# Split weight blocks written over the raw block, six blocks ahead of TensorE

## The reference

```python
for l in range(DEPTH):                                     # DEPTH = 2
    proj = einsum('btd,de->bte', x, w_in[l])               # D_IN = 7168 columns
    ...
    y_conv = conv_mixer(...)                               # 31 taps, 512 channels
    y_hgrn = hgrn2_mixer(...)                              # gated recurrence, 6 heads of 128
    y_ret = retention_mixer(...)                           # 6 heads of 128
    h = einsum('bte,ed->btd', concatenate([y_conv, y_hgrn, y_ret]), w_out[l])
    x = layer_norm(ALPHA * x + h, ...)
    f = square(relu(einsum('btd,df->btf', x, w_ff1[l])))   # 2048 -> 8192
    h = einsum('btf,fd->btd', f, w_ff2[l])                 # 8192 -> 2048
    x = layer_norm(ALPHA * x + h, ...)
```

## Time and profile before

| | |
|---|---|
| time, median of 3 runs | 3781.74 us (3781.71 to 3783.3) |
| span of the profiled execution | 3784.1 us |
| TensorE busy | 3541.0 us (94%) |
| VectorE busy | 2168.7 us (57%) |
| ScalarE busy | 1618.5 us (43%) |
| GpSimd busy | 419.4 us (11%) |
| moved by DMA | 615.57 MB, mean 163 GB/s |

### The profile page before, as it was taken

How to read it: one execution, slowest core, us unless ns; L and a number is a source line. 1 busy time by engine, 2 the same in 40 slices (tenths; PEclk the granted TensorE clock), 3 DMA queues, 4 the chain that set the end, 5 groups by cost and what they waited for, 6 DMA issues and landing times.

```text
span 3784.1 us, 45287 instructions
## 1 busy us (share of the span) xinstructions
PE 3541.0 (94%) x16538; PEld 2940.2 (78%) x16538; DVE 2168.7 (57%) x2397; ACT 1618.5 (43%) x1953; POOL 419.4 (11%) x330
## 2 busy tenths in 40 slices
PE   7899989999999888989899999999999978999979
PEld 6677778887888766777788888888888777788767
DVE  4976564555555587665555545565447544645544
ACT  3444334343434335433444443444445433355543
POOL 0614000000000060140100000000000041000100
PEclk9999999999999999999999999999989889999989
DMA  6444456655565555445566666556646200565534
GB/s 224 137 150 148 163 173 186 195 185 182 185 188 184 165 151 149 134 150 187 203 190 188 192 186 192 185 187 193 194 136 175 87 6 31 165 193 169 160 104 134
DMA packets 310641, 615.57 MB, mean 163 GB/s; under 512 B 19082, under 2 KB 19113, under 8 KB 308539
## 3 DMA queue, kind: packets, MB, share of 16 engines
q1 hardware_dynamic: 306144, 591.73, 50.6%
q0 software_dynamic: 4320, 21.34, 1.8%
HBM read 610.90 MB, written 2.10 MB: 162 GB/s over the span
## 4 chain that ended last, share of the span: by engine, by line
PE 81%; DVE 13%; ACT 4%; issue 2%; DMA 0%; POOL 0%; SPq 0%; DVEq 0%; ACTq 0%
PE ps_unit L252 24%; PE ps_unit L254 24%; PE ps_unit L253 24%; DVE sb_w_lo L236 4%; DVE sb_conv_y L901 2%; PE ps_mix L2324 2%; ACT sb_w_hi L229 2%; PE ps_mix L975 1%; PE ps_mix L376 1%; PE ps_mix L530 1%; DVE sb_h_s L1167 1%; PE ps_mix L1995 1%; PE ps_mix L2322 0%; DMA sb_raw<-in_w_in_dram 0%; PE ps_mix L2679 0%
## 5 line engine op out<-in xcount | busy, mean ns | idle before, releaser
L236 DVE TENSOR_TENSOR sb_w_lo<-sb_raw,sb_w_hi 128x1024 fp32r<-128x1024 f32 x1120 | 1407.7, 1264 | 1311.6 <-ACT sb_w_hi L229 1305.9
L229 ACT ACTIVATE sb_w_hi<-sb_raw 128x1024 fp32r<-128x1024 f32 x1120 | 1183.1, 1060 | 1838.1 <-PE ps_unit L254 1823.6
L252 PE MATMUL ps_unit<-sb_w_hi,sb_a_hi 128*128 128x512 f32 x3456 | 1383.1, 400 | 87.1 <-DVE sb_w_lo L236 56.0
L253 PE MATMUL ps_unit<-sb_w_lo,sb_a_hi 128*128 128x512 f32 x3456 | 1361.4, 394 | 0.0
L254 PE MATMUL ps_unit<-sb_w_hi,sb_a_lo 128*128 128x512 f32 x3456 | 1361.1, 394 | 0.0
L252 PEld LDWEIGHTS ps_unit<-sb_w_hi,sb_a_hi 128*128 128x128 f32 x3456 | 660.1, 191 | 242.9 <-DVE sb_w_lo L236 49.5
L254 PEld LDWEIGHTS ps_unit<-sb_w_hi,sb_a_lo 128*128 128x128 f32 x3456 | 658.5, 191 | 141.3
L253 PEld LDWEIGHTS ps_unit<-sb_w_lo,sb_a_hi 128*128 128x128 f32 x3456 | 660.0, 191 | 132.8
L252 PE MATMUL ps_unit<-sb_w_hi,sb_f_hi 128*128 128x512 f32 x1024 | 399.9, 391 | 0.0
L254 PE MATMUL ps_unit<-sb_w_hi,sb_f_lo 128*128 128x512 f32 x1024 | 398.6, 389 | 0.0
L253 PE MATMUL ps_unit<-sb_w_lo,sb_f_hi 128*128 128x512 f32 x1024 | 398.4, 389 | 0.0
(11 more groups left out here) (455 smaller groups left out, 2142.7 us busy)
## 6 DMA issues: line engine op xcount, KB each, us to landing
sb_raw<-in_w_ff_dram SPq DMA_DIRECT2D x512, 512.0 KB, 3.8
sb_raw<-in_w_in_dram SPq DMA_DIRECT2D x224, 512.0 KB, 3.8
sb_raw<-in_e_w_in_dram SPq DMA_DIRECT2D x112, 512.0 KB, 3.6
sb_raw<-in_o_w_in_dram SPq DMA_DIRECT2D x112, 512.0 KB, 3.7
sb_raw<-in_w_out_dram SPq DMA_DIRECT2D x64, 512.0 KB, 4.4
sb_raw<-in_e_w_out_dram SPq DMA_DIRECT2D x32, 512.0 KB, 4.4
sb_raw<-in_o_w_out_dram SPq DMA_DIRECT2D x32, 512.0 KB, 4.7
sb_raw<-in_e_w_mem_kv_dram SPq DMA_DIRECT2D x16, 512.0 KB, 4.5
```

The lines of the kernel that those rows point to most:

```text
L229: k.nc.scalar.activation(k.w_hi[:, slot], k.raw[:, j], ACT.Copy).then_inc(k.hi_ready, 1)
L236: k.nc.vector.tensor_tensor(k.w_lo[:, slot], k.raw[:, j], k.w_hi[:, slot].bitcast(F32), ALU.subtract).then_inc(k.lo_ready, 1)
L252: k.nc.tensor.matmul(acc, hi[:, kt, tokens], w_hi, start=kt == 0, stop=False)
L253: k.nc.tensor.matmul(acc, hi[:, kt, tokens], w_lo, start=False, stop=False)
```

## The change

The low half of a block is written in place over the raw block, and the high half gets eight slots of its own, in the memory that both halves had before. SyncE's load of a slot now waits for TensorE to have finished the block eight earlier, which was the last reader of the slot. ScalarE's split no longer waits for TensorE: the load that it waits for implies it. The splits stand six blocks ahead of TensorE's place in the program in place of four, and the counts that start the semaphores follow (`block_done` begins at 8, `lo_ready` at 0).

```diff
-HI_SLOTS = 4
+AHEAD = 6
...
     k.raw = sb("raw", 0, [P, BLOCKS, KB, NC])
-    k.w_hi = sb("w_hi", 32 * K, [P, HI_SLOTS, KB, NC], F32R)
-    k.w_lo = sb("w_lo", 48 * K, [P, HI_SLOTS, KB, NC], F32R)
+    k.w_lo = sb("w_lo", 0, [P, BLOCKS, KB, NC], F32R)
+    k.w_hi = sb("w_hi", 32 * K, [P, BLOCKS, KB, NC], F32R)
...
 # sp_unit (and sp_feed_forward alike)
-        sp.wait_ge(k.lo_ready, b0 + (s * BLOCKS + j + 1))
+        sp.wait_ge(k.block_done, b0 + (s * BLOCKS + j + 1))
         sp.dma_start(k.raw[:, j], w[:, KB * j:KB * (j + 1), bass.ds(column, NC)]).then_inc(k.raw_ready[j], 16)
...
 # act_split
     act.wait_ge(k.raw_ready[j], b0 * 2 + 16 * (c // BLOCKS + 1))
-    act.wait_ge(k.block_done, b0 + (c + 1))
-    k.nc.scalar.activation(k.w_hi[:, slot], k.raw[:, j], ACT.Copy).then_inc(k.hi_ready, 1)
+    k.nc.scalar.activation(k.w_hi[:, j], k.raw[:, j], ACT.Copy).then_inc(k.hi_ready, 1)
...
 # dve_split
-    k.nc.vector.tensor_tensor(k.w_lo[:, slot], k.raw[:, j], k.w_hi[:, slot].bitcast(F32),
-                              ALU.subtract).then_inc(k.lo_ready, 1)
+    k.nc.vector.tensor_tensor(k.w_lo[:, j], k.raw[:, j], k.w_hi[:, j].bitcast(F32), ALU.subtract).then_inc(k.lo_ready, 1)
...
 # pe_block
-    pe.wait_ge(k.lo_ready, b0 + (BLOCKS + c + 1))
+    pe.wait_ge(k.lo_ready, b0 + (c + 1))
...
 # split_units; Meanwhile.ahead and the feed-forward loops alike
-            for c in range(HI_SLOTS, HI_SLOTS + BLOCKS):
-                if take and c == HI_SLOTS + BLOCKS - 1:
+            for c in range(AHEAD, AHEAD + BLOCKS):
+                if take and c == AHEAD + BLOCKS - 1:
...
 # wait_unit
-    eng.wait_ge(k.block_done, b0 + (HI_SLOTS + (s + 1) * BLOCKS))
+    eng.wait_ge(k.block_done, b0 + (s + 2) * BLOCKS)
...
 # start of the kernel, ScalarE and VectorE
-            for c in range(HI_SLOTS):
+            for c in range(AHEAD):
...
 # VectorE
-            dve.sem_inc(k.lo_ready, BLOCKS)
...
 # TensorE
-            pe.sem_inc(k.block_done, HI_SLOTS)
+            pe.sem_inc(k.block_done, BLOCKS)
```

More of the change, by code:

```diff
@@ L218, in sp_unit @@
     for j in range(BLOCKS):
-        sp.wait_ge(k.lo_ready, b0 + (s * BLOCKS + j + 1))
+        sp.wait_ge(k.block_done, b0 + (s * BLOCKS + j + 1))
         sp.dma_start(k.raw[:, j], w[:, KB * j:KB * (j + 1), bass.ds(column, NC)]).then_inc(k.raw_ready[j], 16)
 def act_split(act, k, b0, c):
-    j, slot = c % BLOCKS, c % HI_SLOTS
+    j = c % BLOCKS
     act.wait_ge(k.raw_ready[j], b0 * 2 + 16 * (c // BLOCKS + 1))
-    act.wait_ge(k.block_done, b0 + (c + 1))
-    k.nc.scalar.activation(k.w_hi[:, slot], k.raw[:, j], ACT.Copy).then_inc(k.hi_ready, 1)
+    k.nc.scalar.activation(k.w_hi[:, j], k.raw[:, j], ACT.Copy).then_inc(k.hi_ready, 1)
 def dve_split(dve, k, b0, c):
-    j, slot = c % BLOCKS, c % HI_SLOTS
+    j = c % BLOCKS
     dve.wait_ge(k.hi_ready, b0 + (c + 1))
-    k.nc.vector.tensor_tensor(k.w_lo[:, slot], k.raw[:, j], k.w_hi[:, slot].bitcast(F32),
-                              ALU.subtract).then_inc(k.lo_ready, 1)
+    k.nc.vector.tensor_tensor(k.w_lo[:, j], k.raw[:, j], k.w_hi[:, j].bitcast(F32), ALU.subtract).then_inc(k.lo_ready, 1)
 def pe_block(pe, k, b0, c, hi, lo):
-    s, j, slot = c // BLOCKS % 2, c % BLOCKS, c % HI_SLOTS
+    s, j = c // BLOCKS % 2, c % BLOCKS
     if j == 0:
         pe.wait_ge(k.evacuated, b0 + (c + BLOCKS))
-    pe.wait_ge(k.lo_ready, b0 + (BLOCKS + c + 1))
+    pe.wait_ge(k.lo_ready, b0 + (c + 1))
     for n in range(KB):
@@ L250, in pe_block @@
             acc = k.ps_unit[:, s, t, :]
-            w_hi, w_lo = k.w_hi[:, slot, n, :], k.w_lo[:, slot, n, :]
+            w_hi, w_lo = k.w_hi[:, j, n, :], k.w_lo[:, j, n, :]
             k.nc.tensor.matmul(acc, hi[:, kt, tokens], w_hi, start=kt == 0, stop=False)
@@ L309, in __init__ @@
         self.eng, self.k, self.block, self.take = eng, k, block, take
-        self.ahead = 0 if who == "pe" else HI_SLOTS
+        self.ahead = 0 if who == "pe" else AHEAD
         self.first = k.block0[who]
@@ L512, in sp_feed_forward @@
                     src = w2_groups[:, bass.ds(q, 1), rows, (u - 4) * NC:(u - 3) * NC].rearrange("p q kt n -> p (q kt) n")
-                sp.wait_ge(k.lo_ready, b0 + (u * BLOCKS + j + 1))
+                sp.wait_ge(k.block_done, b0 + (u * BLOCKS + j + 1))
                 sp.dma_start(k.raw[:, j], src).then_inc(k.raw_ready[j], 16)
@@ L574, in group @@
         for u in range(FF_UNITS):
-            for j in range(4, 8):
+            for j in range(AHEAD, AHEAD + 4):
                 act_split(act, k, b0, u * BLOCKS + j)
                 if between:
-                    between(u, j - 4)
+                    between(u, j - AHEAD)
             if 1 <= u <= 4:
@@ L582, in group @@
                                        ACT.Copy).then_inc(k.f_hi_ready, 1)
-            for j in range(8, 12):
+            for j in range(AHEAD + 4, AHEAD + 8):
                 act_split(act, k, b0, u * BLOCKS + j)
                 if between:
-                    between(u, j - 4)
+                    between(u, j - AHEAD)
             if u < 4:
@@ L628, in group @@
                                           ALU.subtract).then_inc(k.f_lo_ready, 1)
-            for j in range(8, 12):
-                if u >= 4 and j == 11:
+            for j in range(AHEAD + 4, AHEAD + 8):
+                if u >= 4 and j == AHEAD + 7:
                     residual(dve, k, b0, u, u - 4)
```

## The result

The changed kernel took 3681.23 us (median of 4 runs, 3675.39 to 3684.41), the kernel before 3781.72 us in the same set: a ratio of 0.9736 (95% interval 0.9722 to 0.9749), 100 us less. 80 less were forecast. Lines are numbered one to two lower in the changed kernel: L236 is L235, L229 is L228, L252 to L254 are L250 to L252.

A forecast was written before the change was run, and what follows sets the result against it. TensorE, busy 3541.0 of 3784.1 us, was taken as the bound, so only its waits and lowered clock could be won. Terms summed to 86 us, less 6 gave 80, hence 3702 us; range 3666 to 3756.

The forecast's parts named there:

- rival B: More is won: every term at its upper end, half-clock stretches included, 104 us, 3678 us; chance 0.10.
- The 0.4 us for two semaphores: In the split's clock: a split can begin at D(n-2), TensorE's finish of block n-2, plus load plus about 0.4 us.
- term 2: Convolution: VectorE bounds the taps, whose rate stays; earlier arrival and earlier splits and statistics behind layer 1's taps win 14 us.
- a next link: Over all terms: some of what is won is met by the same chain's next link; 6 us taken off.
- term 6: Inputs of the odd layer: low-half waits, evacuations behind splits and half clock, 11 us won, bounds 5 to 13.
- Term 1: Starts of phases and of the kernel: six slots cover three waits and their half clock, 16 us won, bounds 10 to 18.
- The eight small waits: Within the starts of phases: eight small low-half waits go, 2 us won.
- Terms 3 to 7: Level loops 13.3, retention 12, differential attention 15, odd layer's inputs 11, even layer, delta rule and last evacuation 5 us.
- the signs named: Low-half waits fall to some 25 us, all beside taps; L1167, L2753, L344 waits vanish; loads land near 3.8 us.
- A: Only waits with a low half's name go, with half clock 33 us, 3749 us; chance 0.20.
- C: No change, 3782 us: loads pace the ring, which needs loads of 5.0 us in the mixers; chance 0.05.
- D: Late loads: from 5.0 us a load delays splits; at 5.5 us some 42 points lose, +20, 3802 us; chance 0.07.

The follow-up runs named there:

- the two by two table: Leads of four and six, standing for TensorE's block or waiting for the load alone: 3777.45 and 3751.40 us standing, 3690.66 and 3681.23 us not.
- before_late_load: The kernel before, with SyncE's load waiting for TensorE to have finished the block eight earlier, not for VectorE's low half: 3784.08 us, 1.0003.
- lead4_free: The changed kernel with a lead of four blocks in place of six, ScalarE's split waiting for its load alone: 3690.66 us, 0.9756.
- lead6_stand: The changed kernel, lead of six, with ScalarE's split again waiting for TensorE, for the block six before it: 3751.40 us, 0.9916.
- lead4_stand: The changed kernel with a lead of four and ScalarE's split again waiting for TensorE's block four before it: 3777.45 us, 0.9991.

## Why the prediction was right, point by point

*The mechanism was right, the time nearer to rival B.* The forecast was 3702 us with a chance of 0.58, rival B 3678 with 0.10; measured were 3681. The standing time of the two splitting engines was the larger part of the gain and is shown by the two by two table: taking it away is worth 87 us at a lead of four and 70 at six. The level loop of the changed kernel shows the step as it was worked out: from 11.83 us to 10.85, three blocks and the 24 matmuls. ScalarE's timeline:

```profile
258.42 1.06 ACT L228 ACTIVATE sb_w_hi<-sb_raw 128x1024 fp32r<-128x1024 f32 x1 [4.44 <-DMA sb_raw<-in_w_in_dram]
...
261.02 1.06 ACT L228 ACTIVATE sb_w_hi<-sb_raw 128x1024 fp32r<-128x1024 f32 x1 [0.16 <-DMA sb_raw<-in_w_in_dram]
```

and VectorE's, which stood 4.61 us before the split in a step and stands 0.82:

```profile
262.11 1.23 DVE L235 TENSOR_TENSOR sb_w_lo<-sb_raw,sb_w_hi 128x1024 fp32r<-128x1024 f32 x1 [0.82 <-ACT sb_w_hi L228]
263.25 2.22 DVE L1152 TENSOR_TENSOR sb_h_d<-sb_h_d,sb_proj 128x768 f32<-128x768 f32 x1
265.39 2.58 DVE L1153 TENSOR_TENSOR sb_h_d<-sb_h_d,sb_proj 128x768 f32<-128x768 f32 x1
```

The 0.4 us for two semaphores stood on no row. In the changed kernel's trace a load is issued 0.17 us (median) after the end of TensorE's block, and a waiting split of ScalarE starts 0.02 us after the load lands: 0.2 us in all, so the splits come a little earlier than was worked out.

*What was mis-sized: TensorE's busy time.* The explicit half-clock items of the terms were 5.1 + 1.2 + 1.7 + 6.0 + 3.4 = 17.4 us, the waits 86 - 17 = 69. Measured: 66.7 us of idle time, and 34.9 of busy time, twice the item. The mean granted clock by core shows the larger part: before

```profile
core 0: 3784.1 us, clock 0.968
```

and after

```profile
core 0: 3682.5 us, clock 0.975
```

A clock of 0.968 over 3784.1 us is 242 us at half, 0.975 over 3682.5 is 184: 58 us less at half clock. TensorE was busy in 185 us of them before and in 136 after by the traces, so the clock is worth half of the 49 us, 24.5. The other 10 us, about, are a term that the prediction doesn't have. A block right behind a wait takes longer at the full clock too: six such blocks beside the taps of the kernel before, 18.08 us busy, 3.01 each, against 2.72 in a row.

```profile
124.00:148.00 24.00, 18.08 (x72) 1.00 0.45 132
```

So a wait that goes brings about 0.3 us more than its length, and there were many short ones; the level loop's step is 0.98 us shorter for a wait of 0.73. I had charged the clock only behind a wait that goes; it also changes where waits merely shrink or move: term 2, which had no such item, has 8.6 us of busy time in its 16.8. Some of the 34.9 is chance: before_late_load has within 1.3 us the idle time of the kernel before (its span of 3771.4 less 3527.0 busy is 244.4, against 243.1) and 14 us less busy time at a clock of 0.973.

The 6 us taken off for "a next link" were right in kind and too small (L874, L528 and POOL's L1239, and what L973 grew by, are such links, 12.9 us together); that the idle time came out near the forecast all the same is due to terms that won more waits than counted, term 6 above all (11.2 us of idle time between blocks 992 and 1072, 7.6 counted).

*Term 1, starts of phases* (16 forecast, 12.4 measured): the 2.7 us waits and the half clock behind them went at all three places, 4.4, 4.5 and 4.7 us over the eight blocks around each, where 4.4 each were forecast. The kernel's start won the 1 us forecast, though the first block came 2.1 us late. The eight small waits brought nothing to be seen: the feed-forward stages are 1.2 us slower in the first layer, and at the third place 2.0 us were lost again at once, to the new wait at L528. That TensorE never waits in the feed-forward stages, as the prediction has it, was misread: by its own page it waited 6.3 us there before ("issue", three times), 4.7 now.

*Term 2, convolution* (14, 16.8): the size is luck, the working was wrong. The prediction let the 11.8 us of low-half waits behind the second layer's taps go and those beside the taps stay. It is the other way round: behind the taps there are 12.1 us, and beside them 9.8 are left of 25.2. The taps' rate did stay, 1.05 us of wait in each block that waits, but only five blocks in a layer still do, where 13 and 12 did. Either part of the change alone does most of it: beside the taps 14.3 us are left in lead4_free and 14.4 in lead6_stand. In layer 0, 10.8 us are won between blocks 28 and 36, and most of it is paid back at the taps' end, where nothing is left to hide VectorE (9.7 us lost from 48 to 56). In layer 1 nothing is paid back: 10.7 us are won between 428 and 440. What is lost in layer 0 is the new wait of 6.2 us before L874. The profile calls it "issue", but the instruction waits for the last taps, which end as it starts:

```profile
197.41 1.27 DVE L899 SCALAR_TENSOR_TENSOR sb_conv_y<-sb_conv_u,sb_conv_w,sb_conv_y 128x256 f32<-128x256 f32 x3
198.60 4.62 DVE L235 TENSOR_TENSOR sb_w_lo<-sb_raw,sb_w_hi 128x1024 fp32r<-128x1024 f32 x4
198.79 1.94 PE L874 MATMUL ps_mix<-sb_square,sb_conv_y 128*128 128x128 f32 x8 [6.24 <-issue]
```

*Terms 3 to 7* came within 5.2 us each, nearly all on the side of more: the mixers' waits went whole where I had credited halves (retention's 5.0 and 4.3 us became 3.2 in all). Terms 6 and 7 lie above their upper bounds (16.2 and 8.0 against 13 and 6). Of the signs named, one failed, the low half's waits "all beside taps", and L344's wait shrank from 2.2 to 1.3 us and didn't vanish.

*The rivals.* A (33 us: only waits with a low half's name go) is close to what lead6_stand measures, 32 us, and the changed kernel isn't that. B (104) came nearest. C is refuted by the 3.6 us landing. The 3.2 us that the prediction estimates for a load from the Trainium skill ("DMA: Bandwidth & Descriptors", "Anatomy of one DMA") rest on a fit that the page gives for DMAs issued by GpSimd; these are SyncE's and took 3.6 to 3.8 us, and the sum used the trace. D (late loads) didn't happen. Its point of decision, 5.0 us, lies between what was measured on either side: with 3.6 us the gain is there, and with one block later, 3.6 + 2.7 us between the issue that the change makes and the landing, most of it was gone. Where between them the gain turns wasn't measured. It was priced too high (802 less 782 at 0.5 us for each point): at 1.3 us past the point the time is still 19 us under the kernel before. That fits a lead that keeps its 32 us (lead6_stand 3751 us, one block later 3762, so the later splits cost 10.5) and level loops that have 2.92 us of cover; the shares of the two weren't measured. In-place writing (30 us at worst) cost nothing, by lead4_stand.

## What to carry to other kernels

When an engine waits for a late mixer instruction, look at what stands ahead of it on its own engine: a feeding instruction that waits for the consumer's progress makes everything behind it late, and the consumer then waits under another name. Take the wait away from the feeder and put it on the DMA queue, where nothing is queued behind it. Count how many blocks lie between a load's issue and its use, for the slack is small (one block, 2.7 us, turned 100 us of gain into 19), and expect a lead to be worth only what the bounding engine doesn't have to make up later.

## What had not been expected of the hardware

VectorE's work, once earlier, ran into GpSimd's. In a level step of the kernel before, the factor L1154 took 0.95 us, with GpSimd done before it; in the changed kernel it took 2.22 (L1152 above, from 263.25), beside two GpSimd instructions. Before, GpSimd and then VectorE:

```profile
272.56 1.81 POOL L1062 TENSOR_TENSOR sb_h_d<-sb_h_cum 128x768 f32<-128x768 f32 x1
...
276.13 0.95 DVE L1154 TENSOR_TENSOR sb_h_d<-sb_h_d,sb_proj 128x768 f32<-128x768 f32 x1
```

and GpSimd after:

```profile
262.78 1.87 POOL L1056 TENSOR_TENSOR sb_h_d<-sb_h_cum 128x768 f32<-128x768 f32 x1 [6.60 <-PE ps_mix L973]
264.62 2.54 POOL L1060 TENSOR_TENSOR sb_h_d<-sb_h_cum 128x768 f32<-128x768 f32 x1
```

Of the 32 such instructions of the two layers, all took 0.95 us in the kernel before, none beside GpSimd; in the changed kernel the 10 with no GpSimd instruction beside them took the same, the 22 others 2.2 us on the mean. That is 28 of VectorE's 46 us more of busy time, and used up over half of the 3.8 us that VectorE stood less in a step; the waits for L1165 went all the same.

The same load landed a little sooner when issued by TensorE's pace: 3.6 us against 3.8 for the input projection, with the same bytes. before_late_load has half of it (3.7), so at least that much comes from the later issue and not from the layout; it brought no time by itself. For the output projection's weights (4.4 before, 3.7 after) nothing is shown: the changed kernel run again has 4.2, the lead of five 4.5. The large row loads that GpSimd issues landed later in the changed kernel, 7.6 us against 5.0 for the gains and 10.9 against 7.0 for the shifts, and did so in before_late_load (7.5 and 10.2), whose time is that of the kernel before.

Runs of one kernel differ by the granted clock: of the kernel before's runs beside lead4_free, the fastest took 3773.5 us at 0.972 and the slowest 3788.5 at 0.967.
